# The x columns of a state-space layer computed with tokens on the partitions, and turned by VectorE and DRAM

## The reference, cut to what matters

```python
zxbcdt = x @ w_in                      # 2048 -> 4096 (z) + 4096 (x) + 1024 (B) + 1024 (C) + 64 (dt)
xbc = conv_general_dilated(xbc, conv_w, padding=[(3, 0)], groups=6144) + conv_b   # 4 taps along the tokens
xbc = silu(xbc)
xs, bm, cm = split(xbc)                # 64 heads of 64, 8 groups of 128, 8 groups of 128
y = ssd_chunked(xs, dt, a, bm, cm) + xs * d_skip
y = y * silu(z); y = rms_norm over each group of 512 columns; x @ w_out ...
```

## Time and profile before

| | |
|---|---|
| median of 3 runs | 2069.11 us (2068.75 to 2069.2) |
| the profiled execution's own time | 2068.77 us |
| its span | 2067.0 us |
| TensorE busy | 2061.2 us |
| VectorE busy | 1414.0 us, 68% |
| ScalarE busy | 1112.0 us, 54% |
| granted clock | full throughout |

### The profile page before, as it was taken

The page is one execution under the profiler, slowest core; times in us unless marked ns, Lnnn a source line. Parts: engine busy times, 40 slices in busy tenths (PEclk is TensorE's granted clock), DMA queues, the critical chain, the costliest instruction groups (busy, mean ns, idle before and its releaser), DMA issues.

```text
span 2067.0 us, 26500 instructions
## 1 busy us (share of the span) xinstructions
PE 2061.2 (100%) x10047; PEld 1719.9 (83%) x10047; DVE 1414.0 (68%) x2200; ACT 1112.0 (54%) x1827; POOL 83.9 (4%) x130
## 2 busy tenths in 40 slices
PE   9999999999999999999999999999999999999999
PEld 8888888888888888888888888888888888888887
DVE  7998888888555889965946666555564545655453
ACT  6666667666434555643746666444554334544432
POOL 0111010111001010000100000000000000000000
PEclk9999999999999999999999999999999999999999
DMA  7777777777665679875666666558786666877674
GB/s 280 239 241 227 230 224 230 237 223 239 227 236 173 207 256 282 245 236 173 198 217 211 204 195 190 176 185 244 240 238 214 193 194 206 242 244 243 195 214 132
DMA packets 141551, 453.66 MB, mean 219 GB/s; under 512 B 16416, under 2 KB 35104, under 8 KB 140784
## 3 DMA queue, kind: packets, MB, share of 16 engines
q1 hardware_dynamic: 130896, 412.29, 64.0%
q0 software_dynamic: 10528, 39.67, 6.0%
HBM read 422.48 MB, written 29.43 MB: 219 GB/s over the span
## 4 chain that ended last, share of the span: by engine, by line
PE 99%; ACT 0%; DMA 0%; DVE 0%; issue 0%; SPq 0%; ACTq 0%; DVEq 0%
PE ps L1662 98%; PE ps L1665 1%; DMA xraw<-in_xt 0%; ACT lnt L687 0%; ACT xhl L690 0%; DVE xhl L1006 0%; DVE res L1015 0%; SPq L547 0%; SPq L541 0%; ACTq L266 0%; DVEq L266 0%
## 5 line engine op out<-in xcount | busy, mean ns | idle before, releaser
L1006 DVE TENSOR_TENSOR wlo<-raw,whi 128x1024 fp32r<-128x1024 f32 (+1 forms) x713 | 865.5, 1218 | 554.3 <-ACT whi L690 552.8
L690 ACT ACTIVATE whi<-raw 128x1024 fp32r<-128x1024 f32 (+1 forms) x713 | 753.1, 1058 | 897.0 <-PE ps L1662 886.3
L1662 PE MATMUL ps<-whi,xhl 128*128 128x512 f32 x2624 | 820.2, 391 | 0.6 <-ACT xhl L690 0.5
L1662 PEld LDWEIGHTS ps<-whi,xhl 128*128 128x128 f32 x2624 | 491.4, 188 | 107.1 <-ACT xhl L690 2.3
L1662 PE MATMUL ps<-wlo,xhl 128*128 128x512 f32 x1312 | 507.6, 389 | 0.0
L1662 PEld LDWEIGHTS ps<-wlo,xhl 128*128 128x128 f32 x1312 | 246.4, 188 | 50.1
L1662 PE MATMUL ps<-xhl,whi 128*128 128x512 f32 (+1 forms) x1032 | 251.2, 392 | 0.5 <-DVE xhl L1006 0.5
L1662 PEld LDWEIGHTS ps<-xhl,whi 128*128 128x128 f32 x1032 | 187.8, 189 | 37.2 <-issue 0.8
L1662 PE MATMUL ps<-whi,hhi 128*128 128x512 f32 x512 | 199.2, 389 | 0.0
L1662 PE MATMUL ps<-wlo,hhi 128*128 128x512 f32 x512 | 199.2, 389 | 0.0
L1662 PE MATMUL ps<-whi,hlo 128*128 128x512 f32 x512 | 199.2, 389 | 0.0
(11 more groups left out here) (210 smaller groups left out, 1787.4 us busy)
## 6 DMA issues: line engine op xcount, KB each, us to landing
raw<-in_w SPq DMA_DIRECT2D x256, 512.0 KB, 4.1
raw<-in_w_qkv SPq DMA_DIRECT2D x96, 512.0 KB, 4.3
raw<-in_w_in SPq DMA_DIRECT2D x95, 512.0 KB, 4.2
raw<-in_w_z SPq DMA_DIRECT2D x64, 512.0 KB, 4.1
raw<-in_w_ao SPq DMA_DIRECT2D x64, 512.0 KB, 4.2
raw<-in_w_bi SPq DMA_DIRECT2D x32, 512.0 KB, 3.6
raw<-in_w_gate SPq DMA_DIRECT2D x32, 512.0 KB, 4.9
raw<-in_w_bo SPq DMA_DIRECT2D x32, 512.0 KB, 4.4
```

The source lines that it names most:

```text
L690: return eng.activation(out, x, ACT.Copy, **kw)
L1006: return eng.tensor_tensor(out, x, y, op)
L1662: return eng.matmul(out, x, y, start=start, stop=stop, skip_group_check=True)
```

## The change

The x columns leave the feature units. They get a token unit of their own, `x`, with 8 slots of `w_x` for each group, and only B and C stay in a feature unit (8 of these, not 24). The order in a group is x, B and C, z: x takes 20g to 20g+7, B and C 20g+8 to 20g+11, z 20g+12 to 20g+19. In group 0 the units x and B/C are interleaved (12 slots), and the chunks of the input are fetched at the slots 3, 6 and 9 in place of 2, 4 and 6. `scan_at` stays 20g+19 for g >= 1 and goes from 22 to 23 for g = 0.

The stationary operand of the x unit holds every second token: tile t has the tokens 2q+t. When x is done, VectorE turns both banks in 32x32 squares straight out of PSUM into `xs`; GpSimd stores that in `raw_way` and loads it back as `raw_rows` (features on partitions, 4 runs of 64 tokens for each of 4 blocks). ScalarE writes the last tap and the bias for 4 blocks at once; VectorE adds the other taps. Since the runs of 64 tokens lie apart in `raw_rows`, each tap of a block takes two instructions: one for the tokens within the runs (252 to 244 elements) and a small one for the first s tokens of the runs 1 to 3 (3s elements). `sums` becomes one buffer, and the semaphores of the keys' and the hidden layer's turning are merged (`kh_...`), with counts shifted by 4.

```diff
     for g in range(GROUPS):
-        a, b, c = (features("in", 3 * g + m, "w_in") for m in range(3))
         if g == 0:
-            woven(a, b)
+            a, b = features("in", g, "w_in"), unit("x", g, "w_x", 8 * g, 16)
+            for j in range(4):
+                slots.extend(a[j:j + 1] + b[2 * j:2 * j + 2])
         else:
-            slots.extend(a + b)
-        slots.extend(c)
+            slots.extend(unit("x", g, "w_x", 8 * g, 16))
+            slots.extend(features("in", g, "w_in"))
         slots.extend(unit("z", g, "w_z", 8 * g, 16))
...
-            if i in (2, 4, 6):
+            if i in (3, 6, 9):
...
-    return ended("in", ORDER.index((g, "x3")) // 2) + (8 if g else 11)
+    return ended("x", g) + 12
...
+            def x_values(g):                        # GpSimd; called before the loop for g = 0, then first in each round
+                w.wait_ge(S["row_turned"], 2 * g + 2)
+                eng.dma_start(raw_way[g, :, :], xs[g % 2][:, :, :].rearrange("p j a -> p (j a)")).then_inc(S["row_stored"], 16)
+                w.wait_ge(S["row_stored"], 16 * (g + 1))
+                w.wait_ge(S["x_conv"], 4 * g)
+                blocks = raw_way[g, :, :].rearrange("(i a) (c x) -> c a i x", i=4, c=4)
+                for c in range(4):
+                    eng.dma_start(raw_rows[32 * c:32 * c + 32, :, :], blocks[c]).then_inc(S["row_loaded"], 16)
...
             for g in range(GROUPS):
                 if g:
+                    x_values(g)
                     w.wait_ge(S["y_ps"], 4 * g)
...
+            def in_proj(g):                         # ScalarE, B and C only
+                yield
+                w.wait_ge(S["conv"], 2 * g)
+                copy_others(INDEX["in", g], sums[:, :, :]).then_inc(S["part"], 1)
+                yield 2
...
+                    act(ACT.Identity, bc[g % 2][:, b, :], sums[:, b, :], bias=shift, scale=t[3]).then_inc(S["ev"], 1)
                 yield 3
+                w.wait_ge(S["made"], 6 * g)
+                for b in range(2):
+                    w.wait_ge(S["conv"], 2 * g + b + 1)
+                    act(ACT.Tanh, th[:, b, :], bc[g % 2][:, b, :]).then_inc(S["tanh"], 1)
+
+            def x_values(g):                        # ScalarE
+                X = xs[g % 2]
+                yield 7
+                w.wait_ge(S["row_loaded"], 64 * (g + 1))
+                w.wait_ge(S["cwb"], 1)
+                for j in range(4):
+                    t, shift = taps(4 * g + j)
+                    act(ACT.Identity, X[:, j, :].rearrange("p (i m) -> p i m", i=4), raw_block(j), bias=shift, scale=t[3]).then_inc(S["ev"], 1)
+                yield 4
+                w.wait_ge(S["made"], 6 * g + 2)
+                for j in range(4):
+                    w.wait_ge(S["x_conv"], 4 * g + j + 1)
+                    act(ACT.Tanh, (th if j < 2 else arg)[:, j % 2, :], X[:, j, :]).then_inc(S["tanh"], 1)
...
+            def x_values(g):                        # VectorE
+                u, X = INDEX["x", g], xs[g % 2]
+                yield
+                w.wait_ge(S["z_turned"], g)
+                for t in range(2):
+                    w.wait_ge(S["weights"], END[u, t])
+                    eng.transpose(X[:, :, :].rearrange("p j a -> p (j a)").rearrange("p (c j b t) -> p t j c b", c=4, j=4, t=2)[:, t],
+                                  ps[:, banks(u)[t], :].rearrange("p (j c a) -> p j c a", j=4, c=4)).then_inc(S["row_turned"], 1)
+                yield 7
+                last = {}
+                for s in (1, 2, 3):
+                    for j in range(4):
+                        t, _ = taps(4 * g + j)
+                        z, raw_z = X[:, j, :].rearrange("p (i m) -> p i m", i=4), raw_block(j)
...
+                        stt(z[:, :, s:64], raw_z[:, :, 0:64 - s], t[3 - s], ALU.mult, z[:, :, s:64], ALU.add)
+                        i = stt(z[:, 1:4, 0:s], raw_z[:, 0:3, 64 - s:64], t[3 - s], ALU.mult, z[:, 1:4, 0:s], ALU.add)
...
+                    yield 1 if s < 3 else 2
+                for j in range(4):
+                    w.wait_ge(S["tanh"], 6 * g + j + 3)
+                    stt(X[:, j, :], (th if j < 2 else arg)[:, j % 2, :], 1.0, ALU.add, X[:, j, :], ALU.mult).then_inc(S["made"], 1)
...
+                elif x.stage == "x":
+                    w.wait_ge(S["row_turned"], 2 * n + 2)
...
+                    tokens = left[:, k, :].rearrange("p (q t) -> p t q", t=2)[:, x] if unit.stage == "x" else left[:, k, x * P:x * P + P]
...
                 Bm, Cm = bc[g % 2][:, 0, :], bc[g % 2][:, 1, :]       # TensorE scan
-                w.wait_ge(S["made"], made_at(g, "C"))
+                w.wait_ge(S["made"], 6 * g + 2)
```

More of the change, by code:

```diff
@@ L247 @@
         "ones", "dt_raw", "dt_in", "dt_e", "dt_al", "dt", "dt_t", "dt_tok", "da", "cum_ps", "cum_sb", "decs", "cum_out", "cum_in",
-        "part", "sum", "ev", "conv", "tanh", "made", "z_tanh", "z_made", "z_turned", "z_stored", "z_loaded", "cb_ps", "cb", "x_turned", "x_stored", "x_loaded", "xc", "dec", "mm", "y_ps", "ysum", "gated", "sq", "ssum", "ms", "rr", "rr_ps", "yn",
+        "part", "sum", "ev", "conv", "tanh", "made", "row_turned", "row_stored", "row_loaded", "x_conv", "z_tanh", "z_made", "z_turned", "z_stored", "z_loaded", "cb_ps", "cb", "x_turned", "x_stored", "x_loaded", "xc", "dec", "mm", "y_ps", "ysum", "gated", "sq", "ssum", "ms", "rr", "rr_ps", "yn",
         "y_high", "y_low",
@@ L354, in build @@
         th = rest("th", [P, 2, T])
-        sums = rest("sums", [P, 2, 2, T])
+        raw_rows = rest("raw_rows", [P, 4, 256])
         xc = rest("xc", [P, 2, 512])
@@ L468, in main_and_rest, with taps, raw_block @@
             return ps[:, b:b + 2, 0:T], ps[:, b:b + 2, T:2 * T]
[L470 to L476, removed]
+        def taps(blk):
             return [cwb[:, blk * 4 + k:blk * 4 + k + 1] for k in range(4)], cwb[:, 192 + blk:193 + blk]
-        blocks_of = [ORDER[2 * n:2 * n + 2] for n in range(24)]
+        def raw_block(j):
+            return raw_rows[:, :, 64 * j:64 * j + 64]
         def gate_of(g):
@@ new lines, in in_proj @@
+                w.wait_ge(S["sum"], g + 1)
+                w.wait_ge(S["cb_ps"], g - 1)
+                w.wait_ge(S["cwb"], 1)
+                for b in range(2):
+                    t, shift = taps(32 + 8 * b + g)
+                    act(ACT.Identity, bc[g % 2][:, b, :], sums[:, b, :], bias=shift, scale=t[3]).then_inc(S["ev"], 1)
+                yield 3
+                w.wait_ge(S["made"], 6 * g)
+                for b in range(2):
+                    w.wait_ge(S["conv"], 2 * g + b + 1)
+                    act(ACT.Tanh, th[:, b, :], bc[g % 2][:, b, :]).then_inc(S["tanh"], 1)
@@ L754, in scan @@
             def scan(g):
+                w.wait_ge(S["made"], 6 * g + 6)
                 for h in range(8):
@@ L963, in hidden @@
                     w.wait_ge(S["weights"], END[INDEX["w2", 3], 1])
-                w.wait_ge(S["h_loaded"], 64 * (U + 1))
+                w.wait_ge(S["kh_loaded"], 64 * (4 + U + 1))
                 copy(hidden_columns(hhi, U), h_rows[:, :, :].rearrange("p i (m b) -> p m i b", m=8)).then_inc(S["h_high"], 1)
             side.at(8, time_steps())
-            for n in range(24):
-                side.at(ended("in", n), in_proj(n))
             for g in range(GROUPS):
+                side.at(ended("in", g), in_proj(g))
+                side.at(ended("x", g), x_values(g))
                 side.at(scan_at(g) + 2, scan(g))
@@ L1170, in add_parts, with in_proj @@
                 return tt(ALU.add, out, main, out)
-            def in_proj(n):
-                yield 2 if n else 1
-                w.wait_ge(S["part"], n + 1)
-                add_parts(INDEX["in", n], sums[:, n % 2, :, :]).then_inc(S["sum"], 1)
-                yield 2 if n else 3
+            def in_proj(g):
+                yield 2
+                w.wait_ge(S["part"], g + 1)
+                add_parts(INDEX["in", g], sums[:, :, :]).then_inc(S["sum"], 1)
+                yield 2
                 last = {}
@@ L1754, in product @@
                     right = weight(i, k, p == 1)
-                    q = mul(ps[:, banks(u)[x], :], left[:, k, x * P:x * P + P], right, start=(u, x) not in opened, stop=last)
+                    tokens = left[:, k, :].rearrange("p (q t) -> p t q", t=2)[:, x] if unit.stage == "x" else left[:, k, x * P:x * P + P]
+                    q = mul(ps[:, banks(u)[x], :], tokens, right, start=(u, x) not in opened, stop=last)
                     opened.add((u, x))
```

92 lines of the change are left out of this document (41 added, 51 removed).

## The result

The changed kernel takes 2089.61 us, the median of 4 runs (2087.40 to 2091.07), beside 2069.15 us (2068.75 to 2070.45, 4 runs) before: ratio 1.0097, interval 1.0079 to 1.0114. It is slower. The forecast was 2074.0 us with 2064.5 to 2083.0 as its range. The time lies outside. The profiled execution took 2087.4 us with a span of 2085.6, 18.6 us more than before. I account for those.

A forecast was written before the change was run, and what follows sets the result against it. TensorE, busy for all but 6 us, was taken as the bound, with VectorE's queue in the state-space stage able to make it wait. Form -4.1, six waits +8.7, start +0.3 gave +4.9 us: 2074.0 us, range 2064.5 to 2083.

The forecast's parts named there:

- I take nothing: TensorE's x slots: loading every second token as stationary operand adds no time; a load may get 1.9 times slower unseen.
- the term of the form: TensorE's x slots: token form takes 2.72 us a slot against 2.78, over 64 slots a gain of 4.1 us.
- The upper bound of 9 us: TensorE's x matmuls: strided loads at 0.24 us would add 0.012 us to each of 768; as a rival, chance 0.09.
- Not in group 1: TensorE's scan of group 1: no wait for B and C, as group 0's scan runs four visits late.
- over 5 us of cover: GpSimd's DRAM trip of x: takes about 12 us, wanted 16.3 + 2.3 us after its start, the turn taking 1.3.
- the bad case: DRAM trip of x: its cover shrinks to about 1 us if VectorE is late by 4.
- a rival: DRAM trip of x: rows land 2 us beyond the cover, holding ScalarE, 7 x 2 = 14 us, 2088; chance 0.08.
- The queue of visits 15 to 18: VectorE, groups 2 to 7: 16.76 us of work in 15.33, so B and C come 1.43 us late, 1.45 with semaphore.
- the small tap: VectorE's convolution of x: twelve small instructions a group, each adding 0.136 us; ends of the range 0.07 and 0.227.
- What is queued behind: ScalarE and VectorE after the late B and C: next `wlo` keeps 4 us of margin, so no second wait.
- The start: TensorE's slot 1: a token slot wants `wlo` in its second matmul and waits 0.2 to 0.3 us once, +0.3.
- the six waits: TensorE at the scans of groups 2 to 7: waits 1.45 us each for B and C, 8.7 us in all.

The follow-up runs named there:

- the changed order: Changed kernel with GpSimd storing x right after z's store, then loading z, then x: 2086.71 us (4 runs), again 2084.11 us (5 runs), median of nine 2084.6.
- the last kernel: Changed kernel with dense operands (even tokens first), B times C one visit later, group 1 two visits later, x stored right after z's store: 2067.78 us, 0.9992.

## Why the prediction was wrong

The direction was right, and the largest term too. Two steps failed, both where I set a cost to nothing.

- **"I take nothing" for the stationary operand.** It costs 0.0067 us a matmul, 5.1 us over 768. The pace shows it in the changed kernel against its contiguous version, the pace and the time in the kernel before with and without the stride. So the term of the form was not -4.1 but +1.1. The upper bound of 9 us had room for it. The Trainium skill, in "SBUF — State Buffer", the section "Door 1: The DMA port swizzle", says that SBUF reads keep full bandwidth as long as two accesses fall on each 16-byte line. For this load it held nearly (193 for 188 ns), but by it the pace of the matmuls would have stayed at 0.227 us, and it went to 0.233. The measurement decides. At stride 4 the load did grow, to 309 ns.
- **"Not in group 1" and "over 5 us of cover".** The cover was worked out for a steady group: from turn to issue 0.3 us, to the loads 5.3. In group 1 the turn of x follows that of z at once, and the issue came 7.1 us after it, behind z's whole trip; the store took 6.5. The trip took 20.9 us where about 12 was forecast (its parts add up to 12.5), and 12.7 was allowed: about 17, less some 4 us by which VectorE was late, which the text had named as the bad case. The rows came 8.2 us late. That cost 5.6 us and about 1.5 at the lower clock; moving group 1 alone gave 7.4 back. I had this as a rival, with 14 us for seven groups and a chance of 0.08; it came in one group. GpSimd's order is a part of it (some 5 us in the median of nine runs, and in two pairs of traces 5.7 and 4.6 us of ScalarE's wait). That the high DMA share (0.92 for 0.77) stretches the store and the loads is what the rows suggest, and no run took the load away by itself.
- **The queue of visits 15 to 18** was right: 16.68 us for 16.76, no gap, the small tap 0.135 for 0.136, the wait 1.41 for 1.45 (1.77 in group 3, which nothing had forecast), all six 8.8 for 8.7 us. Moving B times C and leaving out the small taps each removed all six.
- **What is queued behind** was right for groups 2 to 7: no weight tile comes late. ScalarE's wait for B and C, 44.0 us in nine, stays off TensorE's path.
- **The start** was 0.3 us in the forecast. `wlo` in slot 1 waited 0.29. Slot 1 also began 0.16 later, and one more wait of 0.35 at 89 us was not in the sum.

Measured by its terms, the forecast missed 5.1 us in the form, 7.1 in group 1, 0.7 at the start and at 89 us and 0.1 in the six waits: 13.0 of the 13.7 us by which the span is above the forecast 2071.9.

## What to carry to other kernels

Work out the cover of a new trip in the first groups and not only in a steady one: there the stages overlap otherwise, and one shared queue holds a second trip behind the first. A layout change that puts a stride into the stationary operand can cost more than the instructions it saves; here 3% on each matmul took the whole gain. When work moves ahead of a consumer, sum the producer's queue start to start: this sum was right to 0.1 us.

## What the runs showed that I had not expected

- A matmul of 512 columns whose stationary operand has stride 2 keeps a pace of 0.233 us, not 0.227, with loads of 193 ns. At stride 4 the loads take 309 ns, longer than the pace of 0.235 us that the matmuls keep, so loads overlap one another.
- After a wait of 5.6 us TensorE ran at the lower clock for a moment (1.65 us for a group that takes 0.92). After the six waits of 1.3 to 1.6 us in the same trace it did not, but in the kernel with group 1 later it did, once, after 1.64 us (the granted clock is 0.50 from 253 to 255):

```profile
251.95 1.34 PE L1704 MATMUL ps<-bc 128*128 128x256 f32 x4 [1.64 <-DVE bc L1031]
```

- How long the lower clock lasted differs too: 3.4 us in the changed kernel, about 6.5 in both traces of the changed order, where a part fell into the wait and cost nothing. So the same wait has no fixed price.
- The kernels with a late transfer spread more from run to run: 7.2 us over nine runs with the changed order on GpSimd, 6.4 over six with B times C later, but 1.5 us over eleven in the last kernel, where ScalarE waits 1.2 us for the rows of group 1 and TensorE never for `bc`. The kernel before, which has no such trip, spreads 3.3 us over 27 runs.
